# Weight conversions one position earlier, the ninth slot filled later, and a pause in the weight sums, in a two-layer encoder step

## The chip, the core and the metric

The kernel runs on one core of one Trainium2 chip. The metric is the device time of one launch in microseconds (us). The engines are TensorE (PE in the profile), VectorE (DVE), ScalarE (ACT), GpSimd (POOL) and SyncE (SP), which here only issues transfers. Each runs its own list of instructions in order; they meet at semaphores.

## The reference

Two groups of tokens, 512 of a prompt and 64 of a sample with 512 cached positions, go through two layers that share weights. The kernel keeps them as one array of 576 tokens, features on the partitions, in two halves of 288.

```python
def layer(x, pos, conv_buf, past_ckv, past_kpe, past_pos, ...):
    h = rmsnorm(x, g_pre_mix)
    z = h @ w_in                      # 1024 -> B | C | xin | c_q | c_kv | k_rope | gate_conv | gate_mla
    yc, new_buf = short_conv(c_g * xin, conv_buf, conv_w)
    y_a = b_g * yc
    q = (rmsnorm(cq, g_q) @ w_uq).reshape(B, L, 8, 192)
    ckv_new, kpe_new = rmsnorm(ckv_raw, g_kv), apply_rope(kpe_raw, cos, sin)
    y_b = mla_attention(q_nope, q_pe, pos, ckv_all, kpe_all, k_pos, w_uk, w_uv)
    merged = sigmoid(ga) * y_a + sigmoid(gb) * y_b
    x = x + rmsnorm(merged @ w_o, g_post_mix)
    x = x + rmsnorm(square(relu(rmsnorm(x, g_pre_ffn) @ w1)) @ w2, g_post_ffn)
```

There are 8 heads; head h owns 128 columns of each of B, C, xin and the two gates. All is float32.

## The kernel before

**Precision.** Each float32 matmul is three: every operand is split into a high part (ACT copies it, `pos_hi` for weights) and the rest (DVE subtracts, `pos_lo`), and PE multiplies high by rest, rest by high, high by high (`mm3`, L811 to L813).

**A layer.** First the latent projections, then the heads 0 to 7, then w_o, then the feed-forward part. Heads 0, 1 and 7 are plain: five weight blocks of 128x1024, each used by both halves of the tokens. Heads 2 to 6 are mixed: they compute pairs of projections by seven products on sums and differences of quarters of the weights and of the input. A mixed head uses eight blocks ("positions" `at` to `at + 7`, with `at = HEAD_POS[h]`), half a block for a product. PE goes through it so: products 0 to 3, the head's query, key and value projections (`projections`; in head 2 these come first), products 4 to 6, the scores, two longer half products (`mixed_block`), the turns (transposes of the probabilities, L3527), products 9 to 11, probabilities by values (`attended`), products 12 to 15.

**Softmax.** Beside `mixed_block`, DVE writes the mask (L2404) and finds the row maxima (L2407), ACT takes the exponents (L1487), DVE scales by the reciprocal (L2429), and only then may PE turn. After the turns ACT and DVE split the turned probabilities (`turned_hi` L1494, `turned_lo`), for which `attended` waits.

**Weight slots.** The blocks of the heads go in order through five slots of SBUF, and in part of the run through a sixth, `EXTRA` (slot 8, `w9`), so that up to six are there. `EXTRA_AT` says which positions use it. SP loads a position when PE is through with the one that held its slot before (`pos_before`). All SP transfers are issued in one order, with waits between them, so one late wait holds all behind it. After landing, ACT converts (L1220), then DVE (L2071), in the order of positions and at places written out by hand in `mixed_head` and `plain_head`.

**Small weights.** The per-head latent weights (`small_in`) are loaded when the head before has finished its absorbed queries (`next_small`, L868 to L878), and converted by `small_hi` (L1228). In plain heads `small_hi` stands ahead of `turned_hi`, in mixed heads behind it.

**Weight sums.** The sums of weight quarters that the mixed heads need are made by POOL, with transfers that add in DRAM (`sums_steps`), for both layers during layer 0. Step n copies the blocks of sum n + 1, adds twice to n, once to n - 1 and once, the third addition, to n - 2, after which that sum is complete. SP waits for `sums_third` ahead of the second and the sixth block of each mixed head.

**The reload.** While head 0 runs the normed input is made, in head 1 it is stored to DRAM (`h_store`, L963) and read back in four pieces (`h_load`, L958, semaphores `h_landed[0..3]`) near its end, for the mixed heads.

**Merging.** Each head's result goes out at its end (`merge`, L2363), and SP stores it (`my_kept`, L986). In head 7 SP waits for that store of head 6 to land before it goes on (L990), and after the scores it loads the cache (`cache_n_in`, L999).

## Time and profile before

| what | us |
|---|---|
| median of 3 runs | 1730.63 |
| lowest and highest | 1726.16, 1731.86 |
| the profiled execution | 1731.86 |
| its span in the trace | 1730.1 |
| PE busy in it | 1708.7 |
| DVE, ACT, POOL busy | 1310.8, 854.6, 122.5 |

The profiled execution is the slowest of the three, 1.2 us above the median. 1.8 us of its time lie outside the span. Mean granted clock of PE: 0.996 of full. Matmuls overlap in the trace, so their starts tell more than their lengths. An idle time in brackets is that of the engine ahead of the instruction, with what ended it.

### The profile page before, as it was taken

The page shows a single profiled execution, that of the slowest core. Times are in us where ns is not written, and L with a number is a line of the kernel's source. Part 1 is how long each engine was busy: PE and PEld are TensorE (multiplying, and loading weights), DVE is VectorE, ACT ScalarE, POOL GpSimd, SP SyncE. Part 2 cuts the span into 40 slices and gives each one's busy share as a digit, 9 for nine tenths or more (in the row PEclk, how much of TensorE's full clock was granted, in tenths as well). Part 3 has the DMA queues.
Part 4 walks back from the last instruction along what each step waited for, and adds up shares of the span by engine and source line. Part 5 has one row for each costly group of instructions (what it writes and reads, how often), then busy time and mean ns, then how long its engine had stood idle before and what let it go on. Part 6 is the DMA issues. An engine that isn't in the chain of part 4 may idle for free.

```text
span 1730.1 us, 31892 instructions
## 1 busy us (share of the span) xinstructions
PE 1708.7 (99%) x12735; PEld 1693.8 (98%) x12735; DVE 1310.8 (76%) x2514; ACT 854.6 (49%) x1665; POOL 122.5 (7%) x163
## 2 busy tenths in 40 slices
PE   9999999999999999999999999999999999999997
PEld 9998999999999999999999999999999999999997
DVE  7778787767698876667697897777678887777665
ACT  7625454545365454445366364545446536444452
POOL 1412122221210000000001000000000000000000
PEclk9999999999999999999999999999999999999999
DMA  7899888898743233323124444343533213322231
GB/s 238 202 217 237 210 212 201 205 244 231 157 95 122 70 103 98 89 90 97 56 95 158 156 146 141 112 127 115 171 117 98 92 43 111 98 86 82 78 99 55
DMA packets 90996, 231.54 MB, mean 134 GB/s; under 512 B 9824, under 2 KB 25440, under 8 KB 90848
## 3 DMA queue, kind: packets, MB, share of 16 engines
q1 hardware_dynamic: 71968, 185.45, 33.3%
q0 software_dynamic: 17600, 41.95, 13.6%
q8 instruction: 101, 1.65, 0.4%
q10 hardware_dynamic: 1280, 2.10, 0.3%
q14 instruction: 47, 0.39, 0.1%
HBM read 214.39 MB, written 57.02 MB: 157 GB/s over the span
## 4 chain that ended last, share of the span: by engine, by line
PE 94%; DVE 2%; DMA 2%; ACT 1%; SPq 0%; issue 0%; DVEq 0%; ACTq 0%
PE ring L811 19%; PE ring L813 19%; PE ring L812 19%; PE att L811 11%; PE att L813 11%; PE att L812 11%; DMA cache_n_raw<-cache_n_in 1%; PE att L3527 1%; PE att L806 1%; PE att L805 1%; DMA small_raw<-small_in 1%; PE att L818 0%; ACT rope_s L1291 0%; PE att L3343 0%; DVE xs_lo L2071 0%
## 5 line engine op out<-in xcount | busy, mean ns | idle before, releaser
L811 PE MATMUL ring<-xs_hi,w_lo 128*128 128x288 f32 x1872 | 557.9, 298 | 5.2 <-DVE xs_lo L2744 3.5
L812 PE MATMUL ring<-xs_lo,w_hi 128*128 128x288 f32 x1872 | 552.4, 295 | 0.0
L813 PE MATMUL ring<-xs_hi,w_hi 128*128 128x288 f32 x1872 | 552.3, 295 | 0.0
L2071 DVE TENSOR_TENSOR w_lo<-w_raw,w_hi 128x1024 fp32r<-128x1024 f32 (+1 forms) x364 | 370.6, 1037 | 40.1 <-ACT w_hi L1220 31.2
L811 PEld LDWEIGHTS ring<-xs_hi,w_lo 128*128 128x128 f32 x1872 | 352.7, 188 | 8.4 <-DVE ga L2355 3.7
L812 PEld LDWEIGHTS ring<-xs_lo,w_hi 128*128 128x128 f32 x1872 | 352.7, 188 | 1.4
L813 PEld LDWEIGHTS ring<-xs_hi,w_hi 128*128 128x128 f32 x1872 | 352.6, 188 | 0.0
L813 PE MATMUL att<-f_hi,w_hi 128*128 128x288 f32 x960 | 283.2, 295 | 0.0
L812 PE MATMUL att<-f_lo,w_hi 128*128 128x288 f32 x960 | 282.9, 295 | 0.0
L811 PE MATMUL att<-f_hi,w_lo 128*128 128x288 f32 x960 | 282.6, 294 | 0.0
L811 PEld LDWEIGHTS att<-f_hi,w_lo 128*128 128x128 f32 x960 | 180.4, 188 | 0.0
L812 PEld LDWEIGHTS att<-f_lo,w_hi 128*128 128x128 f32 x960 | 180.4, 188 | 0.0
L813 PEld LDWEIGHTS att<-f_hi,w_hi 128*128 128x128 f32 x960 | 180.4, 188 | 0.0
L1212 ACT ACTIVATE w_hi<-w_raw 128x1024 fp32r<-128x1024 f32 x98 | 102.0, 1054 | 82.2 <-DMA w_raw<-blocks_in 82.1
L1220 ACT ACTIVATE w_hi<-w_raw 128x1024 fp32r<-128x1024 f32 x118 | 122.8, 1052 | 12.5 <-DMA w_raw<-blocks_in 10.3
L2923 DVE TENSOR_TENSOR my<-att,my 128x288 f32<-128x288 f32 x160 | 70.9, 451 | 67.5 <-PE att L813 67.5
L813 PE MATMUL ring<-mix_hi,w_hi 128*128 128x288 f32 x384 | 113.5, 295 | 0.0
L811 PE MATMUL ring<-mix_hi,w_lo 128*128 128x288 f32 x384 | 113.1, 295 | 0.0
L812 PE MATMUL ring<-mix_lo,w_hi 128*128 128x288 f32 x360 | 105.9, 294 | 0.0
L811 PE MATMUL ring<-turn_hi,w_lo 128*128 128x288 f32 x320 | 94.9, 296 | 0.0
L812 PE MATMUL ring<-turn_lo,w_hi 128*128 128x288 f32 x320 | 94.4, 295 | 0.0
L813 PE MATMUL ring<-turn_hi,w_hi 128*128 128x288 f32 x320 | 94.3, 295 | 0.0
(342 smaller groups left out, 3186.5 us busy)
## 6 DMA issues: line engine op xcount, KB each, us to landing
w_raw<-blocks_in SPq DMA_DIRECT2D x195, 512.0 KB, 3.6
weight_sums<-blocks_in POOLq DMA_DIRECT2D x80, 256.0 KB, 7.4
w_raw<-blocks_in SPq DMA_DIRECT2D x62, 256.0 KB, 4.2
weight_sums<-blocks_in POOLq DMA_DIRECT2D x20, 512.0 KB, 5.3
weight_sums<-weight_sums POOLq DMA_DIRECT2D x40, 256.0 KB, 7.7
w_raw<-weight_sums SPq DMA_DIRECT2D x20, 512.0 KB, 4.6
w_raw<-weight_sums SPq DMA_DIRECT2D x40, 256.0 KB, 3.9
small_raw<-small_in SPq DMA_DIRECT2D x16, 320.0 KB, 4.1
```

The source lines that it names most:

```text
L805: pe.matmul(out, both, keys[1], start=False, stop=False)
L806: return pe.matmul(out, both, keys[0], start=False, stop=True)
L811: pe.matmul(out, w[1], x[0], start=first, stop=False)
L812: pe.matmul(out, w[0], x[1], start=False, stop=False)
L813: return pe.matmul(out, w[0], x[0], start=False, stop=last)
L1212: act.activation(hi, raw, ACT.Copy).then_inc(pl.weights_hi, 1)
L1220: act.activation(hi, raw, ACT.Copy).then_inc(pl.weights_hi, 1)
L2071: return dve.tensor_tensor(out, a, hi.bitcast(F32), ALU.subtract)
L2923: dve.tensor_tensor(dst, src, dst, ALU.add).then_inc(pl.w2_free, 1)
L3527: last = pe.transpose(att[:, to:to + P], pl.probs[:, PO[t] + P * j:PO[t] + P * (j + 1)], ident)
```

## The change

It has five parts; none adds or removes arithmetic.

1. `EXTRA_AT` starts five positions later, at 15, 21, 27, 33, 39 instead of 10, 16, 22, 28, 34, and the first use of the slot is loaded behind position 9 instead of behind position 4. So block 10 is no longer loaded ahead of the others in head 0; positions 10 to 14 are loaded one position later each, and positions 40 to 44 one earlier.
2. In the mixed heads ACT and DVE convert one position further ahead: up to `at + 10` instead of `at + 9`. Ahead of the row maxima stand four conversions in each mixed head; before there were two in head 2 and three in the others. Behind them stand four instead of five.
3. `small_hi` stands ahead of `turned_hi` in the mixed heads too, and one conversion ahead of both.
4. Head 7 begins with one conversion instead of two.
5. POOL waits for the last piece of the reload in layer 0 ahead of step 5 of the sums.

```diff
--- before.py
+++ after.py
@@ -98,7 +98,7 @@
     HEAD_POS.append(HEAD_POS[-1] + (8 if is_mixed(head) else N_HEAD))
     HEAD_BANKS.append(HEAD_BANKS[-1] + (16 if is_mixed(head) else 2 * N_HEAD))
 POSITIONS = HEAD_POS[-1]
-EXTRA, EXTRA_AT = 8, tuple(range(HEAD_POS[FIRST_MIXED], POSITIONS, N_HEAD + 1))[0:N_EXTRA]
+EXTRA, EXTRA_AT = 8, tuple(range(HEAD_POS[FIRST_MIXED] + N_HEAD, POSITIONS, N_HEAD + 1))[0:N_EXTRA]
 assert (POSITIONS - N_EXTRA) % N_HEAD == 0
 NBW = NBC + POSITIONS - N_HEAD * HEADS
 
@@ -110,7 +110,7 @@
 def pos_before(q):
 
     same = [p for p in range(q) if pos_slot(p) == pos_slot(q)]
-    return same[-1] if same else q - N_HEAD - 1
+    return same[-1] if same else HEAD_POS[FIRST_MIXED] - 1
 
 
 def weight_loads():
@@ -168,7 +168,7 @@
 
 
 N_SUMS = DEPTH * 2 * MIXED
-BEFORE_KEYS = 2
+BEFORE_KEYS, AFTER_RELOAD = 2, 5
 
 
 def my_row(pl, k):
@@ -1144,6 +1144,8 @@
         def sums_steps(n0, n1):
 
             for n in range(n0, n1):
+                if n == AFTER_RELOAD:
+                    pool.wait_ge(pl.h_landed[3], 16)
                 if n < N_SUMS:
                     pool.wait_ge(pl.sums_copied, 48 * (n + 1))
                 if 1 <= n <= N_SUMS:
@@ -1516,7 +1518,6 @@
                     next_weight(0)
 
                 if h == HEADS - 1:
-                    next_weight(-2)
                     next_weight(-1)
                 if h % 2 == 0:
                     rx_root(1)
@@ -1606,8 +1607,6 @@
                     values_hi(h, 1)
                     if h == FIRST_MIXED:
                         normed_hi(2)
-                    else:
-                        pos_hi(L, at + 3)
                     query_hi(h)
                     rotary_sample(h)
 
@@ -1616,31 +1615,34 @@
                     pos_hi(L, at + 3)
                     normed_hi(3)
                     snapshot(0)
+                    pos_hi(L, at + 4)
+                    pos_hi(L, at + 5)
+                    pos_hi(L, at + 6)
                 else:
                     snapshot(0)
-                    pos_hi(L, at + 2)
+                    pos_hi(L, at + 3)
+                    pos_hi(L, at + 4)
                     if h % 2 == 0:
                         even_projections()
                     else:
                         query_hi(h)
-                        pos_hi(L, at + 3)
                         keys_hi(h)
+                    pos_hi(L, at + 5)
+                    pos_hi(L, at + 6)
                 absorbed_hi(h)
-                pos_hi(L, at + 4)
                 eng.wait_ge(pl.conv_in, L * MIXED + h - FIRST_MIXED + 1)
                 apart()
                 conv_begin(h)
                 exponents(h)
-                pos_hi(L, at + 5)
+                pos_hi(L, at + 7)
+                small_hi(L, h + 1)
                 turned_hi(h)
                 snapshot(1)
-                pos_hi(L, at + 6)
-                small_hi(L, h + 1)
-                pos_hi(L, at + 7)
                 pos_hi(L, at + 8)
                 eng.wait_ge(pl.ring_free, freed(L, r_mixed(h, 10)))
                 act.activation(pl.gb[:, cols(0)], pl.gb[:, cols(0)], ACT.Tanh, scale=0.5)
                 pos_hi(L, at + 9)
+                pos_hi(L, at + 10)
                 eng.wait_ge(pl.ring_free, freed(L, r_mixed(h, 14)))
                 act.activation(pl.ga[:, :], pl.ga[:, :], ACT.Tanh, scale=0.5).then_inc(pl.gated, 1)
                 eng.wait_ge(pl.ring_free, freed(L, r_mixed(h, 15)))
@@ -2501,7 +2503,6 @@
                         next_weight(0)
 
                 if h == HEADS - 1:
-                    next_weight(-2)
                     next_weight(-1)
                 if h % 2 == 0:
                     for half in range(2):
@@ -2661,8 +2662,6 @@
                     values_lo(h, 1)
                     if h == FIRST_MIXED:
                         head_mix_lo(2)
-                    else:
-                        pos_lo(L, at + 3)
                     query_lo(h, 0)
                     query_lo(h, 1)
 
@@ -2674,26 +2673,29 @@
                     first_difference(0)
                     normed_head_lo(2)
                     second_sum(0)
+                    pos_lo(L, at + 4)
                     normed_head_lo(3)
+                    pos_lo(L, at + 5)
                 else:
                     upper_left(0, pl.cv[:, cols(0)])
+                    pos_lo(L, at + 3)
                     first_difference(0)
                     second_sum(0)
-                    pos_lo(L, at + 2)
+                    pos_lo(L, at + 4)
                     if h % 2 == 0:
                         even_projections()
                     else:
                         query_lo(h, 0)
                         query_lo(h, 1)
-                        pos_lo(L, at + 3)
                         keys_lo(h)
+                    pos_lo(L, at + 5)
                 conv_state(h)
                 lower_left(0, pl.u[:, 2:2 + NH])
                 conv_first_half()
+                pos_lo(L, at + 6)
                 lower_right(0, pl.v2[:, :])
                 upper_right(0, pl.cv[:, cols(1)])
                 conv_second_half()
-                pos_lo(L, at + 4)
 
                 row_maxima(h)
                 absorbed_lo(h, pl.rest)
@@ -2701,21 +2703,20 @@
                 probabilities(h)
                 src = ready(7)
                 dve.tensor_tensor(pl.u[:, 0:NH], src, pl.cv[:, 0:NH], ALU.mult).then_inc(pl.ring_free, 1)
-                pos_lo(L, at + 5)
+                pos_lo(L, at + 7)
                 src = ready(8)
                 dve.tensor_tensor(pl.u[:, NH:NP_], src[:, 0:NP_ - NH], pl.cv[:, NH:NP_], ALU.mult)
                 dve.tensor_tensor(pl.u[:, NP_:NT], src[:, NP_ - NH:NH], pl.cv[:, NP_ + 2:NT + 2], ALU.mult) \
                     .then_inc(pl.ring_free, 1)
                 turned_lo(h)
-                pos_lo(L, at + 6)
                 small_lo(h + 1)
                 upper_left(1, pl.gb[:, cols(0)])
+                pos_lo(L, at + 8)
                 first_difference(1)
-                pos_lo(L, at + 7)
                 second_sum(1)
-                pos_lo(L, at + 8)
+                pos_lo(L, at + 9)
                 lower_left(1, pl.ga[:, cols(0)])
-                pos_lo(L, at + 9)
+                pos_lo(L, at + 10)
                 lower_right(1, pl.ga[:, cols(1)])
                 upper_right(1, pl.gb[:, cols(1)])
```

DVE, head 2, from the second sum of the products to the mask. `w_lo` are weight conversions, `head_v`, `u`, `cv` the products' combinations, `xs_lo` the reloaded input. Before:

```order
L2071 TENSOR_TENSOR xs_lo<-xs_lo_raw,xs_hi 128x4x288 [waits h_hi]
L2437 MEMSET u 128x2
L2438 COPY u<-consts 128x2
L2628 TENSOR_TENSOR u<-ring,head_v 128x288 [waits ring_free,ring_full]
L2643 TENSOR_TENSOR u<-u,cv 128x288 [waits ring_free]
L2632 TENSOR_TENSOR head_v<-ring,head_v 128x288 [waits ring_full]
L2634 TENSOR_TENSOR head_v<-head_v,ring 128x288 [waits dve_own]
L2639 TENSOR_TENSOR cv<-head_v,ring 128x288 [waits ring_free,ring_full]
L2647 TENSOR_TENSOR u<-head_v,cv 128x224 [waits ring_free]
L2648 TENSOR_TENSOR u<-head_v,cv 128x64
L2071 TENSOR_TENSOR w_lo<-w_raw,w_hi 128x1024 [waits weights_hi]
L2404 MEMSET att 64x64 [waits scored] x4
```

One conversion, the last thing ahead of the mask; another stands five rows above this piece. The same stretch now (lines are shifted by one or two):

```order
L2073 TENSOR_TENSOR w_lo<-w_raw,w_hi 128x1024 [waits weights_hi]
L2073 TENSOR_TENSOR xs_lo<-xs_lo_raw,xs_hi 128x4x288 [waits h_hi]
L2073 TENSOR_TENSOR w_lo<-w_raw,w_hi 128x1024 [waits weights_hi]
L2439 MEMSET u 128x2
L2440 COPY u<-consts 128x2
L2629 TENSOR_TENSOR u<-ring,head_v 128x288 [waits ring_free,ring_full]
L2644 TENSOR_TENSOR u<-u,cv 128x288 [waits ring_free]
L2073 TENSOR_TENSOR w_lo<-w_raw,w_hi 128x1024 [waits weights_hi]
L2633 TENSOR_TENSOR head_v<-ring,head_v 128x288 [waits ring_full]
L2635 TENSOR_TENSOR head_v<-head_v,ring 128x288 [waits dve_own]
L2640 TENSOR_TENSOR cv<-head_v,ring 128x288 [waits ring_free,ring_full]
L2648 TENSOR_TENSOR u<-head_v,cv 128x224 [waits ring_free]
```

Three conversions stand here instead of one, so two more than before come ahead of the mask, which follows one instruction further down.

SP, from head 0's result to the small weights of head 2. `w_raw` is a slot of the weights. Before:

```order
L859 DMA w_raw<-blocks_in 128x1024
L986 DMA my_kept<-my 128x576 [waits merged]
L949 DMA w_raw<-weight_sums 128x1024 [waits sums_third,ring_full,h_made]
L963 DMA h_kept<-x 128x1728
L954 DMA w_raw<-blocks_in 128x512 [waits ring_full]
L954 DMA w_raw<-weight_sums 128x512
L963 DMA h_kept<-x 128x1728
L868 DMA small_raw<-small_in 128x640 [waits absorbed]
```

Now:

```order
L986 DMA my_kept<-my 128x576 [waits merged]
L859 DMA w_raw<-blocks_in 128x1024 [waits ring_full,h_made]
L963 DMA h_kept<-x 128x1728
L949 DMA w_raw<-weight_sums 128x1024 [waits sums_third,ring_full]
L963 DMA h_kept<-x 128x1728
L868 DMA small_raw<-small_in 128x640 [waits absorbed]
```

The first block's load has gone from the top, and the later ones have moved down by one position.

ACT, head 2, from the row maxima's exponents on. Before:

```order
L1487 ACTIVATE probs,rs<-att,nmx,rows 128x512
L1220 ACTIVATE w_hi<-w_raw 128x1024 [waits slot4]
L1494 ACTIVATE probs_t_hi<-att 128x512 [waits turned]
L1494 ACTIVATE probs_t_hi<-att 128x384 x2
L1588 ACTIVATE head_v<-ring 128x288 [waits ring_free,ring_full]
L1220 ACTIVATE w_hi<-w_raw 128x1024 [waits slot8]
L1228 ACTIVATE small_hi<-small_raw 128x896 [waits small_landed]
```

Now:

```order
L1489 ACTIVATE probs,rs<-att,nmx,rows 128x512
L1222 ACTIVATE w_hi<-w_raw 128x1024 [waits slot2]
L1230 ACTIVATE small_hi<-small_raw 128x896 [waits small_landed]
L1496 ACTIVATE probs_t_hi<-att 128x512 [waits turned]
L1496 ACTIVATE probs_t_hi<-att 128x384 x2
```

The small weights' conversion, with its wait for a transfer, has moved from behind the turned probabilities to ahead of them.

## Rows read from the trace of the kernel before

**Rows 1.** The page, part 1: busy time, share of the span, instructions of the engines.

```profile
PE 1708.7 (99%) x12735; PEld 1693.8 (98%) x12735; DVE 1310.8 (76%) x2514; ACT 854.6 (49%) x1665; POOL 122.5 (7%) x163
```

**Rows 2.** Waits of PE over the whole span: us in total, times, longest.

```profile
PE att L811 <- DVE probs_t_lo L2071: 3.6, 1, 3.6
PE ring L811 <- DVE xs_lo L2744: 3.5, 1, 3.5
PE att L3527 <- DVE probs L2429: 1.8, 1, 1.8
```

**Rows 3.** Stretches of PE: length, busy time, granted clock, DMA share, GB/s.

```profile
138.60:141.60 3.00, 3.00 (x15) 0.50 0.69 199
...
387.60:391.00 3.40, 3.38 (x27) 1.00 1.01 375
...
408.00:411.50 3.50, 3.50 (x17) 0.53 0.19 36
```

**Rows 4.** ACT in time, head 1, layer 0: start, us, instruction, idle before.

```profile
133.49 1.70 ACT L1228 ACTIVATE small_hi<-small_raw 128x1792 fp32r<-128x1792 f32 x1 [8.06 <-DMA small_raw<-small_in]
```

**Rows 5.** Line 873 on SP: the last transfer of head 2's small weights.

```profile
L873 SPq DMA_DIRECT2D small_raw<-small_in x1: 504/504/504, 122.6 to 122.6; - x1
...
DMA to landing us min/median/max: 10.9/10.9/10.9
```

**Rows 6.** The stretch ahead of head 1's wait: busy times, clock, DMA share, GB/s.

```profile
118.00:134.00 16.00, 15.83 (x116) 15.37 (x115) 8.69 (x22) 4.68 (x12) 2.47 (x3) 1.00 0.99 254
```

**Rows 7.** DVE in time, head 2, layer 0.

```profile
163.35 1.21 DVE L2071 TENSOR_TENSOR w_lo<-w_raw,w_hi 128x1024 fp32r<-128x1024 f32 x1
...
170.67 1.21 DVE L2071 TENSOR_TENSOR w_lo<-w_raw,w_hi 128x1024 fp32r<-128x1024 f32 x1
171.90 0.45 DVE L2404 MEMSET att<- 64x64 f32 x4
172.26 1.61 DVE L2407 TENSOR_REDUCE mx<-att 128x1 f32<-128x128 f32 x4
...
176.94 1.27 DVE L2429 TENSOR_SCALAR probs<-probs,ri 128x128 f32<-128x128 f32 x4
```

**Rows 8.** PE in time, head 2: the last score matmul, and the turns.

```profile
171.75 0.40 PE L806 MATMUL att<-kpe_hi,q_pe 128*128 128x512 f32 x1
...
178.35 1.25 PE L3527 MATMUL att<-consts,probs 128*128 128x128 f32 x10
```

**Rows 9.** DVE in time, head 3, layer 0: the last memset of the row maxima.

```profile
211.21 0.11 DVE L2404 MEMSET att<- 64x64 f32 x1 [0.47 <-PE att L806]
```

**Rows 10.** DVE in time, head 2, layer 1: the memsets of the row maxima.

```profile
1027.95 0.46 DVE L2404 MEMSET att<- 64x64 f32 x4
```

**Rows 11.** ACT in time, the end of head 6 and head 7 ahead of its exponents.

```profile
358.02 1.06 ACT L1220 ACTIVATE w_hi<-w_raw 128x1024 fp32r<-128x1024 f32 x1 [2.89 <-DMA w_raw<-blocks_in]
...
379.12 1.06 ACT L1220 ACTIVATE w_hi<-w_raw 128x1024 fp32r<-128x1024 f32 x1 [2.04 <-DMA w_raw<-blocks_in]
```

**Rows 12.** The chain that ended last, in time: start, us, what.

```profile
379.51 17.79 DMA cache_n_raw<-cache_n_in
```

**Rows 13.** POOL in time: step 5's first copy, and layer 0's last third addition.

```profile
138.15 0.75 POOL L1129 DMA_DIRECT2D weight_sums<-blocks_in  x1 [6.28 <-DMA weight_sums<-weight_sums]
...
305.14 0.83 POOL L1142 DMA_DIRECT2D weight_sums<-weight_sums  x1 [7.48 <-issue]
```

**Rows 14.** SP in time, head 6, layer 0: the sixth block's sum and the next.

```profile
318.93 2.86 SPq L954 DMA_DIRECT2D w_raw<-weight_sums  x2
```

**Rows 15.** Line 873 on SP: the last transfer of head 6's small weights.

```profile
L873 SPq DMA_DIRECT2D small_raw<-small_in x1: 749/749/749, 295.6 to 295.6; - x1
...
DMA to landing us min/median/max: 7.6/7.6/7.6
```

**Rows 16.** ACT in time, head 5, layer 0: the turned probabilities.

```profile
302.12 0.60 ACT L1494 ACTIVATE probs_t_hi<-att 128x512 fp32r<-128x512 f32 x1 [2.07 <-PE att L3527]
```

**Rows 17.** PE in time, head 5, layer 0: the first matmul on them.

```profile
306.68 0.40 PE L811 MATMUL att<-probs_t_hi,v_lo 128*128 128x512 f32 x1
```

## The prediction

> **What bounds the kernel now.** I read the page's busy times first. PE is busy 1708.7 of the span's 1730.1 us, the next engine 76% [rows 1]. So only what makes PE wait, or slows its clock, moves the end. PE's waits over the span come next. Three are long, all in layer 0 [rows 2]: 3.6 us for head 1's turned probabilities, 1.8 us for head 7's scaled probabilities, 3.5 us for the last part at the end of head 7. Third, the windows of PE behind them: after 3.6 us without a matmul the granted clock is 0.50 for about 3 us, after 3.5 us it is 0.53 for 3.5 us, after 1.8 us it stays 1.00 [rows 3]. 0.50 is the lower of TensorE's two levels, 1.2 GHz, against 2.4. Half speed costs 3.00 × 0.50 = 1.5 us in the first stretch and 3.50 × 0.47 = 1.6 us in the other. The long waits therefore cost 5.1 and 5.1 us, the short one 1.8.
>
> The mixed heads have no such wait, and there the list in time must be read instead. In head 2 the last score matmul starts at 171.75 and ends about 172.15; DVE reduces at 172.26 and scales until 176.94 + 1.27 = 178.21, and PE turns at 178.35 [rows 7, 8]. The chain from scores to turns leaves 0.14 us. Whatever delays the row maxima by more than that stops PE. It is the tightest place in the program, and the change moves conversions right ahead of it.
>
> **The conversions ahead of the row maxima: the main term.** In head 2 DVE does its last conversion at 170.67 to 171.88 and the first memset follows at 171.90 with no idle time; in layer 1 the memsets at 1027.95 have none either [rows 7, 10]. All DVE instructions of head 2 from about 153 stand end to end, so nothing absorbs a conversion. Two more now stand there. One costs 1.21 us alone, and 1.14 (163.35 to 164.49, the next instruction of that stretch) when its tail overlaps: 2.28 to 2.42 us. The maxima wait that much; less the 0.14 spare, PE waits 2.2 us ahead of the turns, in each layer: +4.4 us. Low end: 0, if conversions, `xs_lo` and combinations overlap better than now. High end: 2.4 a layer, and with the clock falling behind it, as behind 3.5 us but not behind 1.8, 1.6 more: 4.0 a layer. 2.2 is nearer to 1.8, so I take it without the clock. PE does not get it back, as it has no other wait in that stretch that would shrink. In heads 3 to 6 one conversion more stands there. In head 3 DVE has an idle 0.47 us before the last memset [rows 9], and shorter waits for PE and for ACT ahead of it, so one of 1.2 fits if those give 0.6 more: 0, at most 1.2 − 0.47 − 0.1 = 0.6 a head, or 0.6 × 8 = 5 us over both layers. I take 0, since most of those waits are for work that the new order has ready earlier. Four conversions instead of five behind the turns shorten a part in which nobody waits: 0.
>
> **Head 1, layer 0: the gain.** ACT's conversion of the small weights of head 2 starts at 133.49, after 8.06 us idle for the transfer [rows 4]. It stands ahead of the turned probabilities, which PE had ready to split some 6 us before, so PE waits. The last of these transfers was issued at 122.6 and took 10.9 us, in a stretch where the DMA engines are busy 0.99 of the time and move 254 GB/s [rows 5, 6]. The change takes one 512 KB block out of the queues ahead of it, 0.52 MB / 254 GB/s = 2.1 us of the common stream, if the queues were full from that block on. They are full from 118, but were not all the way since 100, so I take 0.9 of the 2.1 us. POOL's pause takes more away, but step 5's first copy starts at 138.15 [rows 13], behind this wait: nothing here. PE's wait goes from 3.6 to 2.7. Whether the clock falls behind 2.7 us lies between the 1.8 and the 3.5 of the rows; I take that it doesn't (−1.5). The term is −2.4 us. Bounds: 0 (the transfer lands as before) to −5.1 (all gone).
>
> The Trainium skill, "DMA: Bandwidth & Descriptors", section Queues, rings and completion order, says that a DMA engine alternates between the queue rows for which it has work, a packet at a time, and takes the descriptors of one queue in ring order. By it a block taken out of SP's own queue, which stands in the same ring ahead of the small weights, brings them earlier by its whole service, and not by a part of it. The share of 0.99 [rows 6] agrees that this stretch is saturated, but no row shows how it is divided. By the rule the landing would come the full 2.1 us earlier, and the sum below would be 1.2 us lower.
>
> **Head 7, layer 0.** Its two conversions at the turn of head 6 wait for blocks: ACT at 358.02 after 2.89 us [rows 11]. The conversion of `at + 10` now stands in head 6 and not in head 7, so head 6's merge comes later by a block's arrival, about 2 us, and its store too. SP waits for that store and then issues the block that ACT converts at 379.12 [rows 11], which is what holds head 7's row maxima. The 1.8 us wait grows to 3.8 if all of it comes through. The end of head 7 is set by another thing: the cache's load starts when head 7's scores are through, at 379.51, and lands 17.79 us later [rows 12]; PE resumes behind it, not behind its own work. Hence the one wait grows by what the other shrinks: +2.0, −2.0. The lower clock behind the end goes (−1.6), and behind the first comes half as likely (+0.8); the load may land 0.2 later. Term: −0.6; bounds −3 (cover reached and clock kept) and +3 (both waits with the clock drop).
>
> **POOL's pause.** Step 5 starts at 138.15 now [rows 13] and would wait for the reload, which DVE begins to split at about 153: 15 us later, and each later step with it. Its last third addition of layer 0 is issued at 305.14 [rows 13], so the tenth sum is complete near 325 instead of 311. SP asks for it at the sixth block of head 6, 318.93 [rows 14], so SP stands still 5 to 7 us. ACT and DVE need that block only at about 333, and a load takes some 5 us: 0. The reload may land sooner; the same place in layer 1, without sums beside it, has no shorter PE time, and none of PE's waits is for the reloaded input: 0. Bounds −0.5 and +4.
>
> **Small weights ahead of the turned probabilities.** In head 5 the turned probabilities are split from 302.12 and PE takes them at 306.68 [rows 16, 17], with 2.5 us to spare. The small weights for head 6 were issued at 295.6 and took 7.6 us [rows 15]: they land at 303.2, so ACT would start 1.1 late, convert for about 1.7, hence 2.8 later than now: 0.3 to 0.5 us of PE wait; 0 elsewhere, where they land long before. I take 0 in the sum, since fewer blocks stand ahead of them now.
>
> **Sum.** +4.4 − 2.4 − 0.6 = +1.4. The profiled execution took 1731.86, its span 1730.1; so 1733.3 for a like execution. That is 1.2 above the median of the runs, 1730.63, so for a median: 1732.0 us.
>
> **The rivals.**
> A. Head 2 does not stall: the two conversions hide, because DVE waits less in its products, and head 1's and 7's gains stay: −3.0, 1727.6. For it: the work of DVE in head 2 could run earlier if ACT's halves do. Against it: no idle time on DVE [rows 7].
> B. Head 1 gains nothing: the transfers land as late as now, because the saved block was through by 118. Then +4.4 − 0.6 = +3.8, or +5 if head 7's clock falls in full behind its new wait: 1734.4 to 1735.6. For it: 15 us between 100 and the wait. Against it: rows 6's full stretch.
> C. Slower: ACT waits for small weights ahead of the turned probabilities in head 5 (and 3) of layer 0. The place is ACT's queue in those heads. It decides once they land later than 302.12 + 2.5 − 1.7 = 302.9. With 7.6 us [rows 15] it costs 0.4; with the 10.9 us of rows 5 they land at 306.5, PE waits 3.6 us and loses 1.5 of clock: +5.1, so 1737.1. For it: POOL's sums are shifted into this stretch. Against it: one block fewer in the queue.
> D. The late sums hold SP long enough that head 6's blocks come late. It decides from about 333 − 5 = 328 on, 3 us later than I expect the sum; each further us costs one. With steps that take 6 us more in all: +3 us, 1735.0.
>
> **Numbers.** My forecast 50%, with a range of its own from 1729.5 to 1734.5; A 12%, B 15%, C 15%, D 8%. What a measurement can tell from no change is 0.3%, 5.2 us: below 1725.4 is faster, above 1735.8 slower. Faster needs A with the whole of head 1's 5.1 us, half of A and a bit of the forecast: 7%. Slower are most of C, a third of B and of D: 20%. The rest, 73%, is within. The range is 1727.5 to 1737.5.
>
> **What the changed profile would show.** The waits of PE: turns behind DVE's scaled probabilities in head 2 of both layers, about 2.2 us each, with four conversions and no idle time ahead of the memsets; head 1's wait for `probs_t_lo` near 2.7 and the window behind it at full clock; head 7's 1.8 near 3.8 and its end near 1.5. POOL's step 5 at about 153, its last third addition near 320, and SP waiting at head 6's sixth block. I am wrong in the main if head 2's turns have no wait (A), if head 1's small weights land at 133.5 again (B), or if a wait for the turned probabilities appears in a mixed head (C).

## The result and the profile after

| | before | changed |
|---|---|---|
| median of 10 runs, us | 1728.14 | 1737.40 |
| lowest, highest | 1723.54, 1735.60 | 1732.80, 1743.01 |
| profiled execution | 1731.86 | 1734.08 |
| PE busy in it | 1708.7 | 1708.8 |
| PE's mean granted clock | 0.996 | 0.996 |

The ratio is 1.0052, interval [1.0032, 1.0072]. The same kernel, run again later beside others, gave 1.0074 [1.0042, 1.0105]. So it is slower by about 9 us. The median lies 0.1 us inside the stated range, and beyond the 0.3% that I called no change; slower had 20%, no change 73%. The two profiled executions differ by 2.2 us only: the one of before took 3.7 more than its median, the changed one 3.3 less. Each trace is a single execution, so the two show only 2 of the 9 us.

PE's long waits now (us in total, times, longest), which answer to [rows 2]:

```profile
PE att L3528 <- DVE probs L2431: 6.3, 3, 2.4
PE att L811 <- DVE probs_t_lo L2073: 2.4, 2, 1.7
...
PE ring L811 <- DVE xs_lo L2745: 0.9, 1, 0.9
```

Two of the three waits for the scaled probabilities are in head 2, the idle time in brackets (last score matmul and turns of layer 0, turns of layer 1; [rows 8]):

```profile
168.65 0.40 PE L806 MATMUL att<-kpe_hi,q_pe 128*128 128x512 f32 x1
177.38 1.31 PE L3528 MATMUL att<-consts,probs 128*128 128x128 f32 x10 [1.98 <-DVE probs L2431]
...
1036.83 1.31 PE L3528 MATMUL att<-consts,probs 128*128 128x128 f32 x10 [1.92 <-DVE probs L2431]
```

Their cause on DVE in layer 0, to be held against [rows 7]: the scores are through at 169.05 and DVE only comes to the memsets 2 us later, with no idle time from 160 on:

```profile
167.86 1.22 DVE L2073 TENSOR_TENSOR w_lo<-w_raw,w_hi 128x1024 fp32r<-128x1024 f32 x1
...
171.06 0.33 DVE L2406 MEMSET att<- 64x64 f32 x4
171.31 1.61 DVE L2409 TENSOR_REDUCE mx<-att 128x1 f32<-128x128 f32 x4
```

Stretches of PE behind a wait (length, busy time, granted clock, DMA share, GB/s), in order: behind head 1's attended, head 2's turns, head 7's turns, the end of head 7; compare [rows 3]:

```profile
137.00:140.00 3.00, 3.00 (x24) 1.00 0.19 68
178.70:181.30 2.60, 2.60 (x13) 0.51 0.90 173
...
390.70:394.20 3.50, 3.46 (x17) 0.56 1.01 366
409.20:412.70 3.50, 3.46 (x26) 1.00 0.68 208
```

The low clock has left head 1 and the end of head 7, and has come behind head 2's and head 7's turns. ACT in head 1, in head 5 and ahead of head 7's exponents [rows 4, 16, 11]:

```profile
130.98 1.70 ACT L1230 ACTIVATE small_hi<-small_raw 128x1792 fp32r<-128x1792 f32 x1 [5.23 <-DMA small_raw<-small_in]
...
305.03 1.70 ACT L1230 ACTIVATE small_hi<-small_raw 128x1792 fp32r<-128x1792 f32 x1 [4.61 <-DMA small_raw<-small_in]
306.64 1.34 ACT L1496 ACTIVATE probs_t_hi<-att 128x512 fp32r<-128x512 f32 x3
...
382.24 1.06 ACT L1222 ACTIVATE w_hi<-w_raw 128x1024 fp32r<-128x1024 f32 x1 [2.70 <-DMA w_raw<-blocks_in]
```

POOL's step 5 and the third addition of the tenth sum; it is issued 6.8 us later than before, not the 15 that I had forecast [rows 13]:

```profile
149.75 0.75 POOL L1129 DMA_DIRECT2D weight_sums<-blocks_in  x1 [28.02 <-DMA xs_lo_raw<-h_kept]
...
311.89 0.83 POOL L1142 DMA_DIRECT2D weight_sums<-weight_sums  x1 [6.44 <-issue]
```

When the starts of the same matmuls are set beside each other, the changed execution is ahead of that of before (−) or behind it (+) by: −2.5 us at head 1's attended (137.38 to 134.87), −4.1 behind the stretch that now has the full clock, −3.3 at head 2's start, +0.6 behind head 2's turns and the slow stretch there, +2.2 at head 5's attended (306.68 to 308.92), +4.4 behind head 7's turns, +0.4 at the end of layer 0, +2.4 behind layer 1's head 2.

### The profile page after: what moved, and what is told of

It reads as the page before. It is cut to its first block, busy times and chain, and to the rows that moved or that the text cites. A ratio compares the mean times of both kernels' runs of the same rounds, so it can differ in the third digit from the quotient of the medians.

```text
span 1732.3 us, 31894 instructions
## 1 busy us (share of the span) xinstructions
PE 1708.8 (99%) x12735; PEld 1693.2 (98%) x12735; DVE 1309.6 (76%) x2514; ACT 857.6 (50%) x1665; POOL 122.2 (7%) x163
## 4 chain that ended last, share of the span: by engine, by line
PE 90%; DVE 5%; DMA 3%; ACT 1%; issue 1%; SPq 0%; DVEq 0%; ACTq 0%
PE ring L811 18%; PE ring L813 18%; PE ring L812 18%; PE att L811 11%; PE att L813 11%; PE att L812 11%; DMA w_raw<-blocks_in 1%; DMA small_raw<-small_in 1%; PE att L3528 1%; DVE w_lo L2073 1%; PE att L806 1%; PE att L805 1%; DVE xs_lo L2073 0%; ACT probs L1489 0%; DVE turn_lo L2073 0%
```

## The experiments

Each kernel was run in five rounds beside the kernel before on one chip, which gave 6 to 12 runs of each; ratios are to that kernel, whose medians in the three groups were 1727.40, 1726.82 and 1727.05. 0.1% is 1.7 us. The first group, of four, was run together; its first three undo one part each.

**Head 2 alone put back.**

```diff
                     pos_hi(L, at + 4)
-                    pos_hi(L, at + 5)
-                    pos_hi(L, at + 6)
                 ...
                 exponents(h)
-                pos_hi(L, at + 7)
+                late = h == FIRST_MIXED
+                pos_hi(L, at + (5 if late else 7))
```

(This is ACT; `at + 6` and `at + 7` follow behind the turned probabilities, and DVE has the same order, with `at + 4` ahead of the row maxima.)

> The changed kernel with head 2 alone put back: one of its conversions ahead of the products' end and one ahead of the row maxima, the other two behind them; nothing else is undone. Theory (head 2 stall is a cost of its own): the two waits of PE ahead of head 2's turns, 2.3 us in layer 0 and 2.2 in layer 1, are gone, and with them the lower clock behind the first (1.4 us); the time falls by 4.4 to 5.9 us against the changed kernel's 1737.4, to about 1732. Rival (the stall only shifts to the next tight place): head 2 has no wait, but the time stays within 1 us of 1737.

Median 1736.71, ratio 1.0052 [1.0033, 1.0071]: no faster. In the trace both waits in head 2 are gone, yet the profiled execution is 2.6 us longer than the changed kernel's. Waits in heads 5 and 6 of layer 0 took their place. PE, at the turns of the two heads:

```profile
303.02 0.47 PE L3538 MATMUL att<-consts,probs 128*128 128x128 f32 x1 [4.18 <-DVE probs L2433]
...
353.81 0.50 PE L3538 MATMUL att<-consts,probs 128*128 128x128 f32 x2 [3.04 <-DVE probs L2433]
```

The chain of waits in head 6 (start, us, what):

```profile
322.48 6.97 DMA weight_sums<-weight_sums
...
331.14 12.10 DMA w_raw<-blocks_in
343.26 1.07 ACT w_hi L1222
...
347.90 1.53 DVE mx L2411 x4
...
353.81 2.21 PE att L3538 x10
```

The tenth sum's last addition lands at 329.45. SP, held for it, then issues four loads within 1.7 us, beside four transfers of POOL's next step, and the last takes 12.1 us. ACT converts that block ahead of head 6's row maxima after 5.43 us of waiting, and PE waits 3.0 us for the turns, after 1.4 us in that head's projections. The longest wait, 4.2 us, is head 5's, and has the same form one head earlier. The eighth sum's addition lands at 278.78 and releases SP and POOL; a load that SP issues at 280.65 takes 11.8 us, and ACT waits 6.8 us for it ahead of the row maxima:

```profile
292.48 1.06 ACT L1222 ACTIVATE w_hi<-w_raw 128x1024 fp32r<-128x1024 f32 x1 [6.80 <-DMA w_raw<-blocks_in]
```

(One of the expectations below gives head 6 the 4.2 us, which are head 5's.) My first theory said nothing of this; the rival, a stall that only moves, holds in the time.

**Small weights behind the turned probabilities again.**

```diff
-                small_hi(L, h + 1)
                 turned_hi(h)
                 snapshot(1)
+                small_hi(L, h + 1)
```

> The changed kernel with the small weights' conversion behind the turned probabilities again in the mixed heads. Theory (they are late in layer 0): head 5's wait for the turned probabilities, 1.9 us in the changed kernel's trace, is gone, and since the timed runs lie 7 us further apart than the two traces do, this wait is longer in most executions, up to 5 us with the clock: the time falls by 2 to 5 us, to 1732 to 1735. Rival (the difference between trace and median comes from elsewhere): it falls by at most 1.9.

Median 1734.82, ratio 1.0050 [1.0030, 1.0070]. Head 5's wait is gone. The median is 2.6 us below 1737.40 and so where the theory had put it; but the kernel before was 0.7 us faster in this group too, and by the ratios, 1.0052 and 1.0050, the gain is 0.3 us. With intervals of 0.2% to either side the run decides between neither.

**No pause.** `AFTER_RELOAD = -1`.

> The changed kernel without POOL's wait for the reload. Theory (the pause costs nothing by itself): within 1 us of 1737. Rival (the pause shifts the sums' transfers into heads 3 to 6 of layer 0 and so delays small weights and blocks there): head 5's small weights land in 7 to 8 us and not in 11.4, its wait goes to under 1 us, and the time falls by 2 to 4 us. Second rival (the pause helps the reload): PE's waits in head 2 ahead of the turns or near 146 to 155 grow, and the time rises by 1 to 3.

Median 1740.29, ratio 1.0065 [1.0040, 1.0090], from six runs: not faster. The first rival fails: head 5's wait is gone, and the time does not fall. The profiled execution, 1731.46, is the fastest of the six, 8.8 us below their median, so it cannot show what makes most of them slow. It does show the second rival's side of the pause, which I had costed at nothing; that the median rose by the 1 to 3 us of this rival is within what the intervals leave open. These are the four loads of the reload, issue and landing, for this kernel:

```profile
L958 SPq DMA_DIRECT2D xs_lo_raw<-h_kept x4: 360/439/1812, 141.6 to 145.2; - x4
...
  ACT xs_hi L1595: 3.0, 1
...
DMA to landing us min/median/max: 10.7/12.7/13.9
```

and for the changed kernel, with the pause:

```profile
L958 SPq DMA_DIRECT2D xs_lo_raw<-h_kept x4: 359/440/509, 140.2 to 143.8; - x4
...
DMA to landing us min/median/max: 4.4/5.0/5.8
```

Without the pause ACT waits 3.0 us for the reload, and PE waits for what ACT and DVE do behind it, 2.08 us, and runs the next 3.4 us at a granted clock of 0.52:

```profile
155.54 0.52 PE L811 MATMUL att<-cqn_hi,small_lo 128*128 128x288 f32 x1 [2.08 <-DVE k_lo L2073]
...
155.80:159.20 3.40, 3.40 (x16) 0.52 1.06 406
```

In the kernel before the reload took 10.1 us in the median and ACT waited only 0.2 us for it; PE, held in head 1, came to that place 2 us later.

**Head 2's conversions alone, on the kernel before.**

```diff
                     snapshot(0)
+                    pos_hi(L, at + 4)
+                    pos_hi(L, at + 5)
+                    pos_hi(L, at + 6)
                 ...
```

(The three are taken out of their old places, and DVE follows.)

> The kernel before with one edit: head 2 converts at + 4, at + 5 and at + 6 ahead of the row maxima, instead of at + 4 alone. Theory: PE waits 2.2 us ahead of head 2's turns in each layer, +4.4 us, with up to 1.5 more a layer where the clock falls: ratio 1.0025 to 1.004. Rival (the stall in the changed kernel needs its other changes): no wait there and no difference.

Median 1731.81 against 1727.40, ratio 1.0022 [1.0010, 1.0034], 3.8 us, and in the trace

```profile
180.81 1.31 PE L3542 MATMUL att<-consts,probs 128*128 128x128 f32 x10 [1.90 <-DVE probs L2436]
...
1036.91 1.31 PE L3542 MATMUL att<-consts,probs 128*128 128x128 f32 x10 [1.91 <-DVE probs L2436]
```

The ratio is a little under the 1.0025 to 1.004 expected, since the clock did not fall. The theory holds: the stall is a cost of its own, and its two waits, 3.8 us, are the whole of it. That undoing it in the changed kernel gains nothing must be due to the other parts. So the next group put each of them alone on the kernel before.

**The ninth slot alone.** The first two hunks of the change.

> The kernel before with the first part of the change alone: the ninth slot starts at position 15 and its first use is loaded behind position 9. Theory (one block fewer ahead of head 1's small weights): head 1's wait is 1 to 3 us shorter, so the ratio is 0.998 to 1.000. Rival (the block's place costs something in heads 2 or 6): ratio 1.001 to 1.003.

Median 1727.09 against 1726.82, ratio 0.9993 [0.9980, 1.0006]: 1.2 us less or nothing. Head 1's wait is 2.9 us in its trace, against 3.6 in that of before; but the other four traces with the old slot have 2.5 to 2.9.

**The order in heads 3 to 6 alone** (with head 7's single conversion at its start). The changed kernel with head 2, the small weights, the slot and POOL as before.

```diff
                     snapshot(0)
-                    pos_hi(L, at + 2)
+                    pos_hi(L, at + 3)
+                    pos_hi(L, at + 4)
                     if h % 2 == 0:
                         even_projections()
                 ...
```

> The kernel before with conversions one position further ahead in heads 3 to 6 and head 7 (parts 2 and 4 of the change), head 2 as before but for one more at its end; the ninth slot, the small weights and POOL as before. Theory (a block that PE doesn't need yet now stands on ACT ahead of the row maxima, and when its transfer is late the turns wait; this is what the experiment with head 2 put back showed in head 6, where ACT waited 5.43 us for it and PE 4.2): runs spread over 8 us or more, ratio 1.002 to 1.004. Rival (only the delayed sums make that block late): ratio within 0.001 of 1, spread as before.

Median 1729.73, ratio 1.0016 [1.0002, 1.0030]: between the theory's 1.002 and the rival's 1.001. The runs spread over 8.7 us, and so did those of the kernel before, so the spread decides nothing. Its trace shows another place for the same mechanism, the projections of head 6 (chain of waits):

```profile
316.20 8.82 DMA w_raw<-blocks_in
325.04 1.06 ACT w_hi L1222
...
328.73 0.47 DVE rope_t L2393
329.24 0.39 PE att L811
```

`at + 4` now stands ahead of the rotation that PE needs; its block lands late, ACT waits 5.11 us, and PE 1.9. A second place is the end of head 4:

```profile
276.49 1.06 ACT L1222 ACTIVATE w_hi<-w_raw 128x1024 fp32r<-128x1024 f32 x1 [6.79 <-DMA w_raw<-weight_sums]
```

This is head 5's block, the one position further ahead. DVE waits for it ahead of its last combinations of head 4, and PE 1.5 us for these. In the kernel with slot and order (below) the same place costs PE 1.6 us, and in none of the traces with the old order is there such a wait.

**The pause alone.** The hunk in `sums_steps`.

> The kernel before with POOL's wait alone. Theory (late sums hurt only where a conversion ahead of the row maxima waits for them): ratio within 0.001 of 1. Rival (SP, held for the tenth sum, delays blocks and small weights of heads 5 and 6 by itself): ratio 1.001 to 1.003, and a wait of PE in head 6.

Median 1727.38, ratio 1.0003 [0.9991, 1.0015]. SP issues the tenth sum's block at 328.90 and not at 318.93 [rows 14], about as late as in the first experiment (329.88), and no wait of PE follows in head 6:

```profile
328.90 1.96 SPq L954 DMA_DIRECT2D w_raw<-weight_sums  x2
```

So the late sum alone costs nothing, as I had predicted.

**The small weights ahead, alone.**

```diff
                 pos_hi(L, at + 5)
+                small_hi(L, h + 1)
                 turned_hi(h)
                 snapshot(1)
                 pos_hi(L, at + 6)
-                small_hi(L, h + 1)
```

(DVE's `small_lo` moves ahead of `pos_lo(L, at + 6)` too.)

> The kernel before with the small weights' conversion ahead of the turned probabilities in the mixed heads, alone. Theory (they land just too late in heads 3 and 5 of layer 0): +0.3 to +2 us, ratio 1.000 to 1.001, with a wait of PE for the turned probabilities in head 5. Rival (they come 3 us and more later in most executions): ratio 1.002 to 1.003.

Median 1730.24, ratio 1.0019 [1.0007, 1.0031], 3.3 us: between theory and rival, nearer to the rival. The trace is of the fastest of the 12 runs, and in it PE waits for the turned probabilities 0.06 us, and 1.0 us at 310.64 for a block that DVE converts behind the small weights. So where the 3.3 us of the median lie is not shown. ACT in head 5, from this trace:

```profile
303.60 1.70 ACT L1228 ACTIVATE small_hi<-small_raw 128x1792 fp32r<-128x1792 f32 x1 [2.97 <-DMA small_raw<-small_in]
```

The one-by-one ratios of all five parts add up to 1.0053, the changed kernel's own. That is a coincidence, as the last group shows. If the parts added up, undoing head 2's or the small weights' would have gained 4 us or 3, and undoing both 7. So a last group put both back, with and without the pause.

**Both put back**, head 2 and the small weights: slot, order and pause stay.

> The changed kernel with two parts undone at once: head 2's conversions back behind the row maxima, and the small weights back behind the turned probabilities. What is left is the ninth slot, the order in heads 3 to 6, and POOL's pause. Theory A (the parts add up as they did one by one on the kernel before: 0.9993, 1.0016, 1.0003): ratio 1.001, runs 1725 to 1735. Theory B (the pause makes blocks late in heads 5 and 6, and the new order makes the row maxima wait for them; neither shows this alone): ratio 1.003 to 1.005, and in the trace a wait of PE over 2 us ahead of head 6's turns or in its projections.

Median 1739.69, ratio 1.0068 [1.0048, 1.0089], from six runs: above what either theory gave, and far from A's 1.001. PE waits 3.3 us ahead of head 5's turns, and 2.1 us in head 6's projections, where B had looked for it.

**The same without the pause.**

> The same without POOL's pause: the ninth slot and the order in heads 3 to 6. Theory A: ratio 1.001, as with the pause, within 0.001. Theory B: 1.001 here and at least 0.002 less than with the pause, with no wait over 2 us ahead of head 6's turns.

Median 1729.78, ratio 1.0014 [0.9999, 1.0029]. Theory B holds: beside the new order the pause costs 9.9 us between the medians, 0.54% ± 0.25%; alone it cost 0.03%. The two profiled executions are 10.5 us apart, so this pair of traces can be compared: 3.8 us lie behind head 5's turns, 7.3 after head 6's projections with the low clock there, 10.0 behind the end of head 7. Head 5, with the pause: SP's loads, and POOL's third addition of the eighth sum and the step that follows it:

```profile
271.89 7.93 SPq L954 DMA_DIRECT2D w_raw<-blocks_in  x3
279.86 0.43 SPq L954 DMA_DIRECT2D w_raw<-weight_sums  x1
...
283.51 1.30 SPq L954 DMA_DIRECT2D w_raw<-blocks_in  x1
...
272.39 0.81 POOL L1142 DMA_DIRECT2D weight_sums<-weight_sums  x1 [7.70 <-issue]
280.04 0.75 POOL L1129 DMA_DIRECT2D weight_sums<-blocks_in  x1 [6.85 <-DMA weight_sums<-weight_sums]
```

The landing at 279.4 releases SP and POOL at once. The load of 283.51 takes 10.27 us, then come ACT and PE's wait (3.3 us, head 5's turns):

```profile
293.80 1.06 ACT L1222 ACTIVATE w_hi<-w_raw 128x1024 fp32r<-128x1024 f32 x1 [5.97 <-DMA w_raw<-blocks_in]
...
PE att L3538 <- DVE probs L2433: 3.3, 1, 3.3
```

Without the pause the eighth sum's addition was issued 16 us earlier, at 255.96, and SP was not held for it. The same load, issued at 282.59, took 5.3 us, and PE waited 0.5 us in all for scaled probabilities. So the load was issued only 0.9 us later with the pause; the difference is in its transfer, which then ran beside the four that POOL had issued from 280.04 and the loads that SP had held back.

**Small weights behind, in head 1**, on the kernel before with the new slot.

```diff
+                if h == 1:
+                    turned_hi(h)
                 small_hi(L, h + 1)
-                turned_hi(h)
+                if h != 1:
+                    turned_hi(h)
```

> The kernel before with the ninth slot's new start and, in head 1 alone, the small weights' conversion behind the turned probabilities. Theory (that conversion's late transfer is all that holds head 1): the wait of 3.6 us and the lower clock behind it, 1.5 us, are gone; ratio 0.996 to 0.998. Rival (the small weights then hold head 2's projections, which need them next): the wait reappears as one of 1 to 3 us near 146, ratio 0.998 to 1.000.

Median 1726.40, ratio 0.9996 [0.9983, 1.0009]. Head 1's wait is gone. Against the trace of before PE is 1.2 us behind at head 1's turns, 4.2 ahead after its attended and 0.8 ahead at head 2's turns: of 5.4 us gained, 2.0 are left. The reload is late now and ACT waits 4.4 us for it:

```profile
L958 SPq DMA_DIRECT2D xs_lo_raw<-h_kept x4: 360/440/1578, 140.1 to 143.7; - x4
...
DMA to landing us min/median/max: 10.6/13.3/15.5
```

and PE waits in head 2's projections:

```profile
PE att L811 <- DVE rx L2457: 1.4, 1, 1.4
PE att L811 <- DVE k_lo L2074: 1.1, 1, 1.1
```

The rival holds, with the reload as the cause more than the small weights.

**The changed kernel again.**

> The changed kernel once more, beside the other three on one chip. Both theories: ratio 1.004 to 1.006. If it lies at 1.004 and the first of these at 1.001, the two parts undone there account for their 0.004 and undoing one alone was only hidden by the spread of the runs.

Median 1736.41, ratio 1.0074 [1.0042, 1.0105], runs from 1731.82 to 1749.49. A little above the 1.004 to 1.006 expected, with an interval that reaches into it; the kernel with two parts undone, at 1.0068, cannot be told from it.

With slot and order in place, four kernels now vary the other parts (ratios to the kernel before):

| | no pause | pause |
|---|---|---|
| head 2 and small weights put back | 1.0014 | 1.0068 |
| head 2 and small weights as in the change | 1.0065 | 1.0052, 1.0074 |

Without the pause the parts add up within the intervals: 1.0014 and the 0.0022 and 0.0019 of head 2 and the small weights alone give 1.0055. With it they do not. Either the pause or the other two bring 0.5%, and the second of them brings nothing more. So no single part, taken out of the changed kernel, gives the 9 us back.

## Why the prediction was right and wrong

The range held the time by 0.1 us, and by luck. I had worked from a median of three runs, 1730.63; against it the range reached from −3.1 to +6.9 us, and the kernel moved by 9.3. The median of ten runs of the kernel before is 2.5 us lower, and that brought the sum back inside. The forecast, +1.4 us, was far off, and so was its own range up to 1734.5. It failed in three terms that I had put at 0: the order in heads 3 to 6, the small weights, and the pause beside them. By its steps:

- **Head 2.** Right in place, cause and size: 2.2 us a layer forecast, 1.98 and 1.92 of idle PE measured, 3.8 us in the time when done alone. The clock, left out of the value and kept in the bound, fell in layer 0 to 0.51 for 2.6 us.
- **Heads 3 to 6.** This is the step that failed first. I costed the conversion that moved ahead of the row maxima by DVE's 1.2 us and its idle time, and took 0. What counted is that a conversion on ACT waits for a transfer, and all behind it waits too. Moved ahead of the row maxima, the rotation and the end of a head, it makes them depend on a block that PE needs much later. Alone it costs 0.16%, [0.02, 0.30].
- **POOL's pause.** "0" was right for the pause alone, and wrong beside slot and order: 0.54% more. In the changed kernel itself, taking it out gained nothing. Rival D named the held SP, but let it decide only when a block is late for its own use, about 328. With the new order it decides as soon as the block is late for the row maxima, and in head 5 as well. I priced each edit against the kernel before, never one against another. The forecast of 15 us for the sums' delay held in the experiments better than in the changed kernel: the tenth sum's third addition, at 305.14 before, came at 311.9 and 315.9 in its two traces, and from 318.2 to 325.2 in the four other kernels with the pause.
- **Small weights ahead.** I took 0; the 0.3 to 0.5 us of the working was the better number, and rival C had the place and the direction: 0.19% alone, 1.7 us of wait in head 5 of one changed trace, none in the other. C's 1737.1 us is nearly the measured time, but by chance: it stood for one wait of 3.6 us with the low clock, on top of the forecast, which neither trace shows.
- **Head 1.** Forecast −2.4; the trace shows −3.3 by head 2. The landing was forecast 0.9 earlier; over the traces ACT starts on the small weights at 133.4 in the mean of five with the old slot and 132.5 in the mean of nine with the new one. That is the 0.9, with a standard error of about 0.5; single traces differ by 3.9. The prediction had worked out a full 2.1 us from the Trainium skill, "DMA: Bandwidth & Descriptors", section Queues, rings and completion order, by which a DMA engine takes the descriptors of one queue in ring order; the traces do not show that much. The wait that the term started from, 3.6 us, was the longest of the five with the old slot: the other four have 2.5 to 2.9, as the slot's move alone has. In the time the slot is worth 0.07% or nothing.
- **Head 7.** Forecast −0.6, about −1.9 in the trace: the turns' wait rose from 1.8 to 2.4 and the clock fell behind it; the end's fell from 3.5 to 0.9 and the clock stayed. The exchange was right, its size not.

What is shown: the costs of the single parts, and that the pause costs 0.5% more beside slot and order. What is only argued: why the pause and the other two parts do not add up. If PE is held in head 2, the row maxima of heads 5 and 6 come later and the late sums hurt less; without that stall the program runs into them. The five traces with order and pause fit, but they differ in the sums' own times too (us; PE's place at head 4's turns against the trace of before):

| kernel | PE at head 4's turns | eighth sum's third addition | PE idle in heads 5 and 6 |
|---|---|---|---|
| head 2 put back | −2.0 | 273.1 | 8.6 |
| both put back | −1.0 | 272.4 | 5.4 |
| changed, second trace | −0.4 | 265.9 | 0 |
| changed | +0.4 | 261.1 | 1.7, small weights |
| small weights put back | +4.7 | 267.3 | 0 |

PE early and sums late go together here, and no run varied one alone. Both traces of the changed kernel are of executions 3.3 and 4.6 us below their medians; what its slower ones, up to 1749.49, wait for is in no trace. That is left open.

No version beat the kernel before: the slot's move, alone or with head 1's small weights moved back, gave 0.9993 and 0.9996, which can't be told from 1.

## What to carry to other kernels

A conversion that is moved forward takes its transfer's wait with it: price it by the landing of its block and by what stands behind it in that queue, not by its own microsecond. Where two edits touch the same chain, one delaying a producer and one bringing its consumer forward, price the pair; each was worth 0.16% or less alone, together, with the ninth slot, 0.7%. And where single executions differ by 5 us and more, one trace each tells where PE waits, but not how much longer the kernel takes: undo parts one at a time and in pairs, and trust the medians.

## What the runs showed of the hardware

When one landing released SP and POOL at once, loads of 256 KB (half a block) took 10.3, 11.8 and 12.1 us; the first took 5.3 in the kernel without the pause. Such long loads are not peculiar to that: each of the 14 traces has one of 10 us or more in its first 400 us, so it matters which block it is. The reload's four transfers landed in 4.8 to 5.3 us in the medians of the six traces with the pause, in which POOL's copies are held back, and in 9.5 to 13.3 in those of the eight others. Behind PE's idle times of 1.98 and 2.08 us the granted clock fell to 0.51 and 0.52, the lower level, for about 3 us. Behind 1.8 us it had not in the trace of before [rows 3], and in the second trace of the changed kernel not behind 2.09 either (head 2's turns, and the stretch behind them):

```profile
178.15 1.31 PE L3528 MATMUL att<-consts,probs 128*128 128x128 f32 x10 [2.09 <-DVE probs L2431]
...
179.50:182.50 3.00, 3.00 (x25) 1.00 0.90 238
```

Nor did it in the kernel with both parts put back behind 3.35 us, ahead of head 5's turns at 304.34:

```profile
305.00:308.00 3.00, 3.00 (x25) 1.00 0.52 154
```

So the length of the wait alone does not decide it; a price for it must stay in the bounds.
